# Gate and up products with a 512-column operand, and four other moves of work, in a two-block layer kernel

## The reference

```
first_block, per layer:
    h = rms_norm(x);  proj = h @ w_in        # NSA, MLA and retention mixers
    x = x + mixed @ w_out
    x = x + square(relu(rms_norm(x) @ w_up)) @ w_down        # width 4096
second_block, per layer:
    mod = c_act @ w_ada + b_ada              # six vectors: shifts, scales, gates
    u = (rmsnorm(x) * (1 + sc1) + sh1) @ w_in
    merged = gates of (pool, short convolution, attention of 8 heads)
    x = x + g1 * (merged @ w_out)
    h2 = rmsnorm(x) * (1 + sc2) + sh2
    x = x + g2 * ((silu(h2 @ w_gate) * (h2 @ w_up)) @ w_down)   # width 2816
```

## Time and profile before

| | |
|---|---|
| median of three runs | 1445.04 us (1444.32 to 1445.49) |
| profiled execution | 1444.84 us, span 1443.0 us |
| TensorE busy | 1425.6 us (99%), 11122 matmuls |
| VectorE busy | 1127.4 us (78%) |
| ScalarE busy | 813.9 us (56%) |
| weights read | 293.56 MB from HBM |

### The profile page before, as it was taken

The page is one execution under the profiler, slowest core; times in us unless marked ns, Lnnn a source line. Parts: engine busy times, 40 slices in busy tenths (PEclk is TensorE's granted clock), DMA queues, the critical chain, the costliest instruction groups (busy, mean ns, idle before and its releaser), DMA issues.

```text
span 1443.0 us, 27500 instructions
## 1 busy us (share of the span) xinstructions
PE 1425.6 (99%) x11122; PEld 1358.3 (94%) x11122; DVE 1127.4 (78%) x2045; ACT 813.9 (56%) x1470; POOL 88.6 (6%) x108
## 2 busy tenths in 40 slices
PE   9999999999999999999999999999999999999999
PEld 9998999889989999988998999999899999999998
DVE  7888788887888787899997688677679757876654
ACT  6585677444576587444656455544465554664442
POOL 0000000000000000000140220000005004000000
PEclk9999999999999999999999999999999999999999
DMA  8432488987234478887454454567444445445451
GB/s 312 168 140 97 173 316 302 334 323 265 98 121 172 147 275 315 313 322 296 176 178 176 183 195 149 204 236 258 178 165 164 177 146 194 156 175 205 176 201 62
DMA packets 44445, 297.43 MB, mean 206 GB/s; under 512 B 6048, under 2 KB 7200, under 8 KB 8992
## 3 DMA queue, kind: packets, MB, share of 16 engines
q1 hardware_dynamic: 42880, 295.13, 55.9%
q0 software_dynamic: 1024, 0.53, 0.2%
q10 hardware_dynamic: 416, 0.02, 0.0%
HBM read 293.56 MB, written 1.05 MB: 204 GB/s over the span
## 4 chain that ended last, share of the span: by engine, by line
PE 79%; DVE 12%; ACT 4%; DMA 3%; issue 1%; POOL 0%; SPq 0%; DVEq 0%; ACTq 0%
PE acc L864 20%; PE acc L866 19%; PE acc L865 19%; PE acc L870 9%; DVE wL L1977 5%; PE acc L871 4%; DMA ring<-stream 2%; ACT wH L1533 2%; PE ps_t L1066 1%; DVE ring L1967 1%; PE ps_s L1053 1%; DMA weights<-region 1%; PE ps_s L1051 1%; PE acc L1156 1%; DVE hL L1991 0%
## 5 line engine op out<-in xcount | busy, mean ns | idle before, releaser
L1977 DVE TENSOR_TENSOR wL<-ring,wH 128x1024 fp32r<-128x1024 f32 x444 | 550.8, 1247 | 214.0 <-ACT wH L1533 204.9
L864 PE MATMUL acc<-hH,wH 128*128 128x256 f32 (+1 forms) x2016 | 577.1, 286 | 4.6 <-DVE wL L1977 2.6
L1533 ACT ACTIVATE wH<-ring 128x1024 fp32r<-128x1024 f32 x444 | 463.8, 1051 | 190.6 <-DMA ring<-stream 78.2
L866 PE MATMUL acc<-hH,wL 128*128 128x256 f32 (+1 forms) x2016 | 568.3, 282 | 0.0
L865 PE MATMUL acc<-hL,wH 128*128 128x256 f32 (+1 forms) x2016 | 566.4, 281 | 0.0
L864 PEld LDWEIGHTS acc<-hH,wH 128*128 128x128 f32 x2016 | 379.7, 188 | 10.2 <-DVE wL L1977 4.8
L865 PEld LDWEIGHTS acc<-hL,wH 128*128 128x128 f32 x2016 | 380.9, 189 | 2.0 <-issue 1.4
L866 PEld LDWEIGHTS acc<-hH,wL 128*128 128x128 f32 x2016 | 381.0, 189 | 0.0
L870 PE MATMUL acc<-aHL,wH 128*128 128x512 f32 x448 | 156.7, 394 | 0.0
L871 PE MATMUL acc<-aHL,wL 128*128 128x256 f32 x448 | 124.3, 282 | 0.0
L1967 DVE SCALAR_TENSOR_TENSOR ring<-ring,onc 128x1024 f32<-128x1024 f32 x96 | 117.0, 1219 | 0.0
(11 more groups left out here) (398 smaller groups left out, 2276.1 us busy)
## 6 DMA issues: line engine op xcount, KB each, us to landing
ring<-stream SPq DMA_DIRECT2D x275, 1024.0 KB, 4.9
cst<-consts SPq DMA_DIRECT2D x1, 1363.0 KB, 15.5
x<-xin SPq DMA_DIRECT2D x4, 256.0 KB, 5.4
ring<-stream SPq DMA_DIRECT2D x2, 512.0 KB, 6.5
out<-x SPq DMA_DIRECT2D x3, 256.0 KB, 6.1
onc<-once SPq DMA_DIRECT2D x1, 516.0 KB, 16.2
weights<-region POOLq DMA_DIRECT2D x32, 16.0 KB, 1.8
v1all<-vec SPq DMA_DIRECT2D x1, 355.0 KB, 9.5
```

Of the source, the lines that this page charges most:

```text
L864: pe.matmul(out, w[0], y[0], start=first, stop=False)
L866: return pe.matmul(out, w[1], y[0], start=False, stop=last)
L1533: act.activation(wH[:, n % SPLIT, :], ring[:, g % RING, half * UNIT:(half + 1) * UNIT], ACT.Copy)\
L1977: TTN(wL[:, n % SPLIT, :], ring[:, g % RING, half * UNIT:(half + 1) * UNIT], wH[:, n % SPLIT, :].bitcast(F32), ALU.subtract).then_inc(lo_r ...
```

## The change

- **Products.** The 38 gate/up units after the first six, in each layer, are made by project_wide: per chunk one matmul of 512 columns, wH·[hH|hL], and one of 256, wL·hH, in place of three of 256. hH and hL become the halves of one buffer hHL. The bank then holds two halves. ScalarE copies the upper one out (gate_low, up_low), VectorE adds the lower (gate_sum, up_sum); tanh, tmp4 and pair2 read the sums. That is two more instructions on either engine for each of 38 pairs. pair_high(2) and pair_low(2) move behind the first of the new steps.
- **Tables.** Tiles of w_ada: block 1 gets one after up 14 and loses those after down 13 and 14, in both layers; block 2, layer 0 has gate 6 and 10 and gate/up 9, 12, 14, 16, 18, 21 in place of gate 4 and 9 and gate/up 12, 15, 18, 21. The rotation steps move from 7, 9, 11, 13 to 8, 9, 12, 14.
- **VectorE, last_product.** gather moves from ahead of the evacuation into the middle of the product.
- **Start.** VectorE's three gathers come before angle steps 4 to 9, not after them.
- **Head of block 2.** ScalarE: wH of one more unit, then root, then take_raw. VectorE: two units split before the root, the third amid hL. The three steps that refine sigma go to the place before y1L.

```diff
-ADA_FIRST = [("up", j) for j in (3, 4, 6, 7, 9, 10, 12, 13, 15)] + [("down", j) for j in (0, 1, 3, 4, 5, 7, 8, 9, 11, 12, 13, 14)]
+ADA_FIRST = [("up", j) for j in (3, 4, 6, 7, 9, 10, 12, 13, 14, 15)] + [("down", j) for j in (0, 1, 3, 4, 5, 7, 8, 9, 11, 12)]
 ADA_AFTER = {
     (1, 0): ADA_FIRST,
     (1, 1): ADA_FIRST,
-    (2, 0): [("gate", 4), ("gate", 9)] + [("gu", j) for j in (12, 15, 18, 21)],
+    (2, 0): [("gate", 6), ("gate", 10)] + [("gu", j) for j in (9, 12, 14, 16, 18, 21)],
...
-ROTATE_AT = {7: 0, 9: 1, 11: 2, 13: 3}
+ROTATE_AT = {8: 0, 9: 1, 12: 2, 14: 3}
...
+        hHL = sb("hHL", [P, 2, KC, PLAIN], F32R)
+        hH, hL = hHL[:, 0, :, :], hHL[:, 1, :, :]
...
+        gate_low, up_low = [sq[:, 3, :], sq[:, 5, :]], [sq[:, 6, :], sq[:, 7, :]]
+        gate_sum, up_sum = [rn[:], sigma[:]], sq[:, 0, :]
...
+            def project_wide(name, ready=None):
+                wh, wl = blocks(next_unit())
+                a = open_acc(name)
+                for c in range(KC):
+                    if ready is not None:
+                        ready(c)
+                    if c == KC - 1:
+                        pe.matmul(a[:, 0:S], wl[:, c, :], hH[:, c, 0:S], start=False, stop=False)
+                    last = pe.matmul(a[:, :], wh[:, c, :], hHL[:, :, c, 0:S], start=c == 0, stop=c == KC - 1)
+                    if c < KC - 1:
+                        pe.matmul(a[:, 0:S], wl[:, c, :], hH[:, c, 0:S], start=False, stop=False)
                 last.then_inc(acc_full, 1)
...
-                    project(name, hs, ready=normed(H2 + KC) if i == 0 else None)
+                    project_wide(name, normed(H2 + KC) if i == 0 else None)
...
@@ ScalarE, head of block 2
+                feed(1 + SPLIT)
+                root(A2, "ss1", L)
                 take_raw(0)
-                root(A2, "ss1", L)
-                feed(1 + SPLIT)
                 if L == 0:
                     act.wait_ge(plain_full, 1)
-                    act.activation(ny[:, 1, :], ps_o[:, 0:S], ROOT, scale=1.0 / D).then_inc(plain_y, 1)
+                    act.activation(sigma[:], ps_o[:, 0:S], ROOT, scale=1.0 / D).then_inc(plain_y, 1)
...
@@ ScalarE, gate/up phase
-                pair_high(2)
                 for n in range(AHEAD // 2, F2):
+                    after = L * (F2 - AHEAD // 2) + (n - AHEAD // 2 + 1)
                     a = full(A2, f"gt{n}", L)
+                    act.activation(gate_low[n % 2], a[:, S:2 * S], ACT.Copy).then_inc(gate_low_ready, 1)
+                    feed(60 + 2 * n + 1 + SPLIT)
+                    if n == AHEAD // 2:
+                        pair_high(n - 1)
                     if n >= 4:
                         act.wait_ge(a2_ready, L * F2 + (n - 3))
-                    act.activation(r4[n % 4], a[:, 0:S], ACT.Tanh, scale=0.5).then_inc(tanh_ready, 1)
-                    feed(60 + 2 * n + 1 + SPLIT)
+                    act.wait_ge(gate_sum_ready, after)
+                    act.activation(r4[n % 4], gate_sum[n % 2], ACT.Tanh, scale=0.5).then_inc(tanh_ready, 1)
+                    a = full(A2, f"up{n}", L)
+                    act.activation(up_low[n % 2], a[:, S:2 * S], ACT.Copy).then_inc(up_low_ready, 1)
                     pair_high(n)
...
@@ VectorE, last_product
+                inner = {n: [name for name in steps if name.startswith(f"dn{n}.")] for n in range(KC)}
                 behind = []
                 for name in steps:
                     n = None if "." in name else int(name[2:])
                     if n is not None:
-                        if norm is not None:
-                            gather(n if n < KC - 1 else KC, norm)
                         evac(n)
                     if name in release and name != f"dn{KC - 1}":
                         feed(release[name] + 1 + SPLIT)
+                    m = int(name[2:].split(".")[0])
+                    if norm is not None and "." in name and name == inner[m][len(inner[m]) // 2]:
+                        gather(m if m < KC - 1 else KC, norm)
...
@@ VectorE, start
                     for step in range(1, 4):
                         angle(step)
                     feed(SIDE)
+                    gather(4, norm1(0, 0))
+                    gather(6, norm1(0, 0))
+                    gather(KC, norm1(0, 0))
                     for step in range(4, 10):
                         angle(step)
                     dve.wait_ge(trig_arg, 1)
-                    gather(4, norm1(0, 0))
-                    gather(6, norm1(0, 0))
-                    feed(SIDE)
-                    gather(KC, norm1(0, 0))
                 feed(SPLIT)
...
@@ VectorE, head of block 2
-                feed(SPLIT)
+                feed(1 + SPLIT)
                 root(A2, "ss1", L, L * Y2N + (Y2 + 1))
                 for c in range(KC):
                     STT(zs[:, c, :], x[:, c, :], raw_gain(L, c), rstd, ALU.mult, ALU.mult).then_inc(h_pre, 1)
-                feed(1 + SPLIT)
                 scale_raw(0)
-                feed(2 + SPLIT)
                 for c in range(KC):
+                    if c == KC // 2:
+                        feed(2 + SPLIT)
                     dve.wait_ge(hh_ready, L * (2 * KC) + H2 + (c + 1))
...
-                if L == 0:
-                    dve.wait_ge(plain_y, 1)
-                    link(TTN(nt, ny[:, 1, :], ny[:, 1, :], ALU.mult))
-                    link(STT(nt, ps_o[:, 0:S], -0.5 / D, nt, ALU.mult, ALU.mult))
-                    link(STT(sigma[:], nt, 1.5, ny[:, 1, :], ALU.add, ALU.mult))
...
                 feed(20 + LEAD + SPLIT)
+                if L == 0:
+                    dve.wait_ge(plain_y, 1)
+                    link(TTN(nt, sigma[:], sigma[:], ALU.mult))
+                    link(STT(nt, ps_o[:, 0:S], -0.5 / D, nt, ALU.mult, ALU.mult))
+                    link(STT(sigma[:], nt, 1.5, sigma[:], ALU.add, ALU.mult))
...
@@ VectorE, gate/up phase
-                pair_low(2)
                 for n in range(AHEAD // 2, F2):
+                    after = L * (F2 - AHEAD // 2) + (n - AHEAD // 2 + 1)
+                    g = full(A2, f"gt{n}", L)
+                    dve.wait_ge(gate_low_ready, after)
+                    TTN(gate_sum[n % 2], g[:, 0:S], gate_low[n % 2], ALU.add).then_inc(acc_drained[A2.bank(f"gt{n}")], 1)
+                    dve.wait_ge(acc_drained[A2.bank(f"gt{n}")], A2.drained(f"gt{n}", L))
+                    dve.sem_inc(gate_sum_ready, 1)
+                    feed(60 + 2 * n + 1 + SPLIT)
+                    if n == AHEAD // 2:
+                        pair_low(n - 1)
                     dve.wait_ge(tanh_ready, L * F2 + (n + 1))
-                    g = psum_of(A2, f"gt{n}")
-                    STT(tmp4[n % 4], r4[n % 4], 1.0, g[:, 0:S], ALU.add, ALU.mult)\
-                        .then_inc(acc_drained[A2.bank(f"gt{n}")], 1)
-                    feed(60 + 2 * n + 1 + SPLIT)
-                    dve.wait_ge(acc_drained[A2.bank(f"gt{n}")], A2.drained(f"gt{n}", L))
+                    STT(tmp4[n % 4], r4[n % 4], 1.0, gate_sum[n % 2], ALU.add, ALU.mult)
                     u = full(A2, f"up{n}", L)
-                    STT(pair2[n % 2], tmp4[n % 4], 0.5, u[:, 0:S], ALU.mult, ALU.mult).then_inc(aT_ready, 1)
-                    dve.wait_ge(aT_ready, L * F2 + (n + 1))
-                    dve.sem_inc(acc_drained[A2.bank(f"up{n}")], 1)
+                    dve.wait_ge(up_low_ready, after)
+                    TTN(up_sum, u[:, 0:S], up_low[n % 2], ALU.add).then_inc(acc_drained[A2.bank(f"up{n}")], 1)
+                    dve.wait_ge(acc_drained[A2.bank(f"up{n}")], A2.drained(f"up{n}", L))
+                    STT(pair2[n % 2], tmp4[n % 4], 0.5, up_sum, ALU.mult, ALU.mult).then_inc(aT_ready, 1)
                     feed(60 + 2 * n + 2 + SPLIT)
                     pair_low(n)
```

More of the change, by code:

```diff
@@ L487, in trn_kernel @@
         wL = sb("wL", [P, SPLIT, UNIT], F32R)
-        hH = sb("hH", [P, KC, PLAIN], F32R)
-        hL = sb("hL", [P, KC, PLAIN], F32R)
+        hHL = sb("hHL", [P, 2, KC, PLAIN], F32R)
+        hH, hL = hHL[:, 0, :, :], hHL[:, 1, :, :]
         BIG = 24 * S
@@ L655, in trn_kernel @@
         tanh_ready = sem("tanh_ready")
+        gate_low_ready, gate_sum_ready, up_low_ready = sem("gate_low_ready"), sem("gate_sum_ready"), sem("up_low_ready")
         a2H_ready = sem("a2H_ready")
@@ L931, in project @@
                     last = split_product(a[:, 0:S], (wh[:, c, :], wl[:, c, :]), y(c), c == 0, c == KC - 1)
+                last.then_inc(acc_full, 1)
+            def project_wide(name, ready=None):
[9 more added lines that the diff above has]
+                        pe.matmul(a[:, 0:S], wl[:, c, :], hH[:, c, 0:S], start=False, stop=False)
                 last.then_inc(acc_full, 1)
```

## The result

The changed kernel takes 1466.68 us (median; 1466.08 to 1468.15) against 1444.68 (1442.54 to 1445.49): 1.0157 times the time before, interval 1.0144 to 1.0170, 22 us slower. The forecast was 1459.5 with a range from 1448 to 1464: the direction and the main cause were right, and the sum was 7 us short.

A forecast was written before the change was run, and what follows sets the result against it. TensorE bounds the kernel before; after the change the VectorE-ScalarE hand-off loop sets the gate/up pace. Gate/up +18.8 and the smaller terms −4.1 make +14.7 on 1444.84: 1459.5 us, range 1448 to 1464.

The forecast's parts named there:

- the loop of VectorE and ScalarE: Gate/up hand-off from one pair2 to the next: 4.79 us grows to 5.71 to 5.83, over TensorE's 5.56.
- two signs of being wrong: No TensorE waits in layer 1's gate/up, or loops with a w_ada tile not 2.3 us longer than those without.
- Rival A: Gate/up loop: dependent steps cost nothing extra, loop 5.45 us, total +2.3, 1447 us; chance .15 for 1444 to 1452.
- The tiles of w_ada: Layer 0's gate/up: six tiles, each adding 2.30 us to the loop, all reaching TensorE: +13.8 us.
- The sum of +18.8 for gate/up: Gate/up phases of both layers together: +16.3 us in layer 0 and +2.5 in layer 1.
- case C: Slower than forecast: layer 0's backlog runs into the down product, or restarting TensorE costs more; above 1464 us, chance .10.
- Terms 5 to 7: TensorE waits cut at the rotation (−2.2 us), the head of block 2 (−0.6) and layer 0's attention (−0.8).
- The rotation's −2.2: Rotation one step later: wL no longer stands behind the wait for rotation data; −2.2 us, from 0 to −2.4.
- case D: Small parts cancel only in part, stalls reappearing at the next wait, loop at its lower price: 1457 to 1459 us.
- The head's −0.6: Head of block 2: the wait on hL is cut by −0.3 us a layer, −0.6 in all, 0 to −1.1.
- The start: Gathers before the angle steps delay the sine and the take that frees TensorE's bank: +1.3 us, −1.1 to +2.3.
- Block 1's end: Two w_ada tiles fewer ahead of it: TensorE's 1.60 us wait for wL goes, −1.8 us, from 0 to −1.8.

The follow-up runs named there:

- the swap: Changed kernel with the up unit's wH ahead of pair_high in ScalarE's gate/up loop (also called the one with wH first): 1438.85 us, ratio 0.9963.
- kept_busy(8): Changed kernel with wH ahead of pair_high, plus 8 unread constant matmuls in TensorE's wait at the start: 1438.42 us, ratio 0.9967.
- kept_busy(18): Changed kernel with wH ahead of pair_high, plus 18 unread constant matmuls in TensorE's wait at the start: 1439.09 us, ratio 0.9964.

## Why the prediction was right and wrong

**What bounds: right.** The prediction's central step, that the loop of VectorE and ScalarE goes from 4.79 to 5.83 and overtakes TensorE, is shown by the rows (5.83) and by the swap, which takes it away and with it 27.8 us. Of its two signs of being wrong neither came: the loops with a tile are 2.3 us longer (8.12), and TensorE's waits in layer 1 are there, .28 in every second unit, though only its weight loads show them. In layer 0 there are six waits of .9 to 1.9 us, one to a tile, not twelve near 2: the two products of a tile lie in one loop. The price of .46 for up_sum and .58 for gate_sum was measured as .45 and .56. Rival A, in which a dependent step costs nothing, falls: tmp4, whose result nobody waits for in the next step, takes .34, up_sum, with a wait for itself behind it, .45, and gate_sum, with a wait and a signal, .56. What costs is the wait, not the semaphore: L2750 of the kernel before signals one and takes .33. The Trainium skill ("VectorE: DVE Perf Modes", The DRAIN you can't avoid) says that a semaphore after each operation costs nothing extra. For the signal alone this case agrees, with that .33; for a step whose successor waits for it, .45, it does not carry over, as the prediction held.

**The tiles of w_ada: right.** A loop with a tile takes 8.12 us, 2.3 over the loop without. Up to up19 five of the six tiles have passed, 11.5 us, and 17 pairs of .13, 2.2: 13.7, and 14.6 were measured. That they were free under the old loop, too.

**The end of the phase: wrong by 2.6.** The sum of +18.8 for gate/up was mis-sized: measured 17.8 in layer 0 and 3.6 in layer 1, 21.4 (16.3 and 2.5 forecast). The sum lacked one step. I counted the loop's lag up to the last wL and took it that the pairs are ready when the down product starts; but the last pair's low part comes 1.7 and 1.3 us after TensorE wants it. The time measured lies where case C had it, above 1464, with a chance of .10. C's ground was a backlog that runs on into the down product; TensorE does wait there, but for a low part of the pairs where C had the splitting of the units, and in both layers.

**Terms 5 to 7: wrong by 3.6.** The rotation's −2.2 did come off at v10, −1.3 in layer 0 and −.9 in layer 1, and 1.1 came back in each layer by g0, .36 at cca and .76 at g0; the text had this as its case D, but only together with the lower price of the loop. The step that failed was to read each wait by itself: the run with the rotation steps alone shows the same sum of nothing and a new wait of .51 us ahead of g0. The head's −0.6 was zero: in layer 1 TensorE still waits .86 us for hL. In the attention the wait of 1.01 went (−1.1), and .5 and .6 us came in its neighbourhood, together zero.

**The start: right in kind, short by .8.** +1.3 forecast, +2.1 measured. The unit starts at 23.49, not 24.2, since the sine came at 20.79 and not 21.59. That is no fault of the shift of 2.26: the trace before had its angle steps .8 us late (L1944 at 16.84; the same step at 16.07 in the kernel with the product alone, whose start is the old one). Against that, the fall of the clock added 1.5. The prediction had no term for the clock.

**Block 1's end: the number met (−1.8; −2.0 measured), the cause not shown.** The wait that the term takes away is not there either, or only .3 us of it, in two of the three other kernels with the old block 1, and not in the changed kernel with the old tiles. That it never shows in the kernels with the new tiles fits a smaller risk of it; how much of the −2.0 is the move and how much chance, the runs leave open.

The four errors, +2.6, +3.6, +0.8 and −0.2, make 6.8 of the 7 us. The small gains were forecast near their upper ends, and all but the one at block 1's end came off at zero; seen afterwards, a range made from the main case with none of them, 1444.84 + 18.8 + 1.3, would have reached 1465, and 1468 with the last pair's wait.

## What to carry to other kernels

Where two engines hand a buffer to and fro, add up the loop from one hand-off back to itself, not the busy time: an instruction added to this loop, or the order in which one of the two engines took up independent work, cost or gave its full length once the loop was longer than TensorE's 5.56 us a pair. Before adding work to such a loop, look for an instruction that waits ahead of one that could run, and change the two: here that turned a loss of 22 us into a gain of 5, and with the old start 7.7. The small waits that were removed here came back at the next places, so a sum of them is best read as an upper bound. And before a wait of 1 to 2 us in one trace becomes a term, look for it in a second execution: here one such wait was all but missing in two of four.

## What was not expected of the hardware

- An idle TensorE of about 2 us was followed by some 3.2 us at the lower level of the clock (0.50 granted, .213 us per 256-column matmul instead of .119) in some executions and not in others: it came after 1.90 us of waiting in the changed kernel and not after 2.55 us in the one with wH first. It came again in the run with the old table, behind the wait of 1.91 us in the attention. In the gate/up phase of layer 0 the granted clock was 0.95 on average; there TensorE was waiting anyway.
- Most of VectorE's operations take longer while GpSimd computes beside them: a wL 1.6 us in place of 1.2, a product of 512 columns 1.0 to 1.2 in place of .69, in the stretch from 734 to 741 us, in both kernels. Not all do: in the changed kernel a wL at 725.72, beside a GpSimd operation of 64x256, took 1.21.
- A matmul of constants in fp32 runs as two instructions for 128 columns: kept_busy(8) shows as 16, 1.95 us, and kept_busy(18) as 36, 4.18 us, .116 each.
- The four transfers of one rotation step, issued within 2 us, land between 1.8 and 6.2 us after their issue (the product alone, from 1097.57).
